# Two plain tiles ahead of the Strassen-like products in the second FFN pass

## What is computed

```python
x = x + gt1 * rms_norm(yx, norm_g[1])                   # yx: mLSTM output
h = rms_norm(x, norm_g[2]) * (1 + sc2) + sh2
u, g = split(h @ w_in)                                  # 1024 -> 2 x 2816
f = (silu(dwconv(g)) * u) @ w_out                       # 2816 -> 1024
x = x + gt2 * rms_norm(f, norm_g[3])
```

## Time and profile before

| | us |
|---|---|
| median of 3 runs (2484.39 to 2489.68) | 2487.13 |
| the profiled execution, its own time | 2494.55 |
| its span in the trace, first to last instruction | 2492.5 |
| PE busy / DVE / POOL / ACT | 2354.7 / 1742.9 / 875.3 / 815.7 |
| mean granted TensorE clock, share of full speed | 0.976 |

### The profile page before, as it was taken

The page is one execution under the profiler, slowest core; times in us unless marked ns, Lnnn a source line. Parts: engine busy times, 40 slices in busy tenths (PEclk is TensorE's granted clock), DMA queues, the critical chain, the costliest instruction groups (busy, mean ns, idle before and its releaser), DMA issues.

```text
span 2492.5 us, 36004 instructions
## 1 busy us (share of the span) xinstructions
PE 2354.7 (94%) x13606; PEld 1926.0 (77%) x13606; DVE 1742.9 (70%) x2193; ACT 815.7 (33%) x1182; POOL 875.3 (35%) x432
## 2 busy tenths in 40 slices
...
DMA packets 106689, 255.08 MB, mean 102 GB/s; under 512 B 8929, under 2 KB 62817, under 8 KB 92129
## 3 DMA queue, kind: packets, MB, share of 16 engines
...
## 4 chain that ended last, share of the span: by engine, by line
PE 78%; DVE 12%; ACT 4%; DMA 3%; issue 2%; POOL 1%; SPq 0%; ACTq 0%; DVEq 0%; POOLq 0%
PE ps L717 17%; PE ps L718 16%; PE ps L719 16%; PE ps L1365 4%; PE ps L1367 4%; PE ps L1366 4%; DVE acc L2822 3%; DVE y_x L2868 2%; PE ps L1115 2%; PE ps L1116 2%; PE ps L1117 2%; PE ps L1268 1%; PE ps L819 1%; PE ps L852 1%; PE ps L754 1%
## 5 line engine op out<-in xcount | busy, mean ns | idle before, releaser
L2953 POOL TENSOR_TENSOR w_lo<-raw,w_hi 128x2048 fp32r<-128x2048 f32 x57 | 266.8, 4681 | 653.0 <-ACT w_hi L1604 293.9
L717 PE MATMUL ps<-hx_hi,w_hi 128*128 128x512 f32 x848 | 338.7, 399 | 2.5 <-ACT mix_out_c L1758 1.0
L718 PE MATMUL ps<-hx_hi,w_lo 128*128 128x512 f32 x848 | 331.8, 391 | 0.0
L719 PE MATMUL ps<-hx_lo,w_hi 128*128 128x512 f32 x848 | 331.5, 391 | 0.0
L2333 DVE TENSOR_TENSOR y_x<-y_x,ps 128x1024 f32<-128x1024 f32 x176 | 214.7, 1221 | 63.0 <-PE ps L719 59.5
L2315 DVE SCALAR_TENSOR_TENSOR acc<-ps,fcv,acc 128x945 f32<-128x945 f32 (+2 forms) x176 | 215.0, 1222 | 37.4 <-ACT acc L1648 16.3
L2822 DVE SCALAR_TENSOR_TENSOR acc<-ps,fcv,acc 128x945 f32<-128x945 f32 (+2 forms) x176 | 215.0, 1222 | 18.6 <-ACT acc L2159 2.7
L2868 DVE TENSOR_TENSOR y_x<-y_x,ps 128x512 f32<-128x512 f32 x304 | 205.2, 687 | 14.1 <-PE ps L719 14.0
L717 PEld LDWEIGHTS ps<-hx_hi,w_hi 128*128 128x128 f32 x848 | 160.2, 189 | 40.3 <-DVE hx_lo L2470 2.5
L719 PEld LDWEIGHTS ps<-hx_lo,w_hi 128*128 128x128 f32 x848 | 160.1, 189 | 34.0
L718 PEld LDWEIGHTS ps<-hx_hi,w_lo 128*128 128x128 f32 x848 | 160.3, 189 | 30.6
...
## 6 DMA issues: line engine op xcount, KB each, us to landing
raw<-in_ffn_w SPq DMA_DIRECT2D x44, 1024.0 KB, 6.6
...
f_raw<-in_ffn_w SPq DMA_DIRECT2D x22, 1024.0 KB, 5.0
modw<-in_modw SPq DMA_DIRECT2D x21, 1024.0 KB, 4.8
raw<-in_mlstm_w SPq DMA_DIRECT2D x14, 1024.0 KB, 5.3
...
```

Of the source, the lines that this page charges most:

```text
L717: pe.matmul(out, whi, hhi, start=first, stop=False)
L718: pe.matmul(out, wlo, hhi, start=False, stop=False)
L719: return pe.matmul(out, whi, hlo, start=False, stop=last)
L2953: pool.tensor_tensor(w_lo[:, slot, 0:2048], raw[:, slot, 0:2048], w_hi[:, slot, 0:2048].bitcast(F32), ALU.subtract)\
```

## The change

The first two tiles are made plainly, with eight multiplications: `first_halves` runs the first token half of gate and up of both tiles (32 steps) while the second half is still being normed, with its sums of squares between them; `second_halves` follows when x12 and x22 exist (another 32 steps). The combinations t1 to t4 are made behind that, mostly on POOL, and are first used in tile 2, which takes the gate-first order and whose weight parts lie in swapped slots (THIRD_SLOT), since the plain tiles still hold the others. `free_at` takes these slots in. SP's first two loads of f_raw and the order of its others change with it. The low part of the gated product of tiles 1 to 20 goes from DVE (`f_low` in `f_tile`) to POOL (`gated_low` in `parts`, behind sum s4). Tile 21 takes the gate-first order. The semaphore bases are moved to fit; they are left out here, as are `plain` (one step: three matmuls of the same 128 x 512 form) and the functions that only take a new name for the order. The diff, cut, in the order SP, PE, ACT, DVE, POOL:

```diff
-FIRST_ORDER = ("g1", "g2", "s1", "s2", "s4", "s3", "u2")
+GATE_FIRST = ("g1", "g2", "s1", "s2", "s4", "s3", "u2")
 ORDER = ("g1", "s1", "s2", "s4", "s3", "g2", "u2")
-MADE_FIRST = FIRST_ORDER
+MADE_THIRD = ("s1", "u2", "g1", "g2", "s2", "s4", "s3")
+PLAIN = 2
...
+PLAIN_PARTS = (("g1", "g2", "s1", "s2"), ("a1", "a2", "b1", "b2"))
+PLAIN_GATE = (2, 0)
+PLAIN_UP = ((1, 1), (5, 4))
+THIRD_SLOT = {"g1": "g1", "g2": "g2", "u2": "u2", "s1": "s4", "s4": "s1", "s2": "s3", "s3": "s2"}
...
 def free_at(name):
-    return max(done_at(True, name), done_at(False, name))
-def made_at(first, name):
-    return (MADE_FIRST if first else ORDER).index(name) + 1
+    return max(done_at(True, name), done_at(True, THIRD_SLOT[name]), done_at(False, name))
...
+sp.dma_start(f_raw[:], a["ffn_w"][FT][:, 0:2048]).then_inc(sem("raw_in0"), 16)
 sp.wait_ge(sem("gated"), 8)
 sp.wait_ge(sem("mo_low"), 1)
 sp.wait_ge(sem("x_out"), 16 * KT)
 sp.dma_start(res_h[:], x_scr[1][:, :, 0:TH]).then_inc(sem("resh_in"), 16)
+sp.wait_ge(sem("lo_in"), PLAIN_LOW + 4)
+sp.dma_start(f_raw[:], a["ffn_w"][FT + 1][:, 0:2048]).then_inc(sem("raw_in0"), 16)
...
-halves_in(1)
-sp.wait_ge(sem("c_shifted"), SECOND["c_shifted"] + KH)
-sp.wait_ge(sem("pre_t"), SECOND["pre_t"] + 18)
+halves_in(2)
+sp.wait_ge(sem("post_done"), posts["x_mlstm"] + 16)
 out_in(0)
+sp.wait_ge(sem("c_shifted"), SECOND["c_shifted"] + 8)
+sp.wait_ge(sem("pre_t"), SECOND["pre_t"] + 2)
 mod_half(0)
-halves_in(2)
...
+def first_halves():
+    for step in range(4 * KT):
+        t, up, k = step // (2 * KT), step // KT % 2, step % KT
+        if step < KT:
+            pe.wait_ge(sem("pre_lo"), lows["x_pre2b"] + k + 1)
+        if k % KH == 0:
+            pe.wait_ge(sem("lo_in"), PLAIN_LOW + 4 * t + 2 * up + k // KH + 1)
+        if t and up and k == 0:
+            pe.wait_ge(sem("act_moved"), PLAIN_MOVED + 1)
+        plain(t, up, 0, k)
+        if step == 1:
+            half_sums("p", 3, KT - 1)
+        if step == 7:
+            pe.wait_ge(sem("sq_p"), 32)
+            half_spread("p", 3)
+        if 14 <= step <= 28 and step % 2 == 0:
+            half_sums("q", 3, (step - 14) // 2)
+    half_spread("q", 3)
+def second_halves():
+    for k in range(KT):
+        pe.wait_ge(sem("pre_lo"), lows["x_pre2b"] + 8 + k + 1)
+        plain(0, 0, 1, k)
+        plain(0, 1, 1, k)
+    pe.wait_ge(sem("act_moved"), PLAIN_MOVED + 2)
+    for k in range(KT):
+        plain(1, 0, 1, k)
+    for k in range(KT):
+        plain(1, 1, 1, k)
...
+    product("g1", made("g1"), third)
     if last:
         pe.wait_ge(sem("mod1_done"), FT)
-    product("g2", made("g2"))
-    pe.wait_ge(sem("dve_moved"), j * 3 + (SECOND["dve_moved"] + 2))
-    product("u2", made("u2"))
+    if third or last:
+        product("g2", made("g2"), third)
+    pe.wait_ge(sem("dve_moved"), j * 3 + (summed - 2))
+    if third:
+        pe.wait_ge(sem("pool_low"), SECOND["pool_low"] + 10)
+    product("s1", made("s1"), third)
+    pe.wait_ge(sem("act_moved"), j * 4 + (moved + 1))
+    if third:
+        pe.wait_ge(sem("pool_low"), SECOND["pool_low"] + 12)
+    product("s2", made("s2"), third)
+    pe.wait_ge(sem("act_moved"), j * 4 + (moved + 2))
+    product("s4", made("s4"), third)
+    pe.wait_ge(sem("act_moved"), j * 4 + (moved + 3))
+    if third:
+        pe.wait_ge(sem("pre_lo"), SECOND["pre_lo"] + 2)
+    product("s3", made("s3"), third)
+    if not (third or last):
+        pe.wait_ge(sem("dve_moved"), j * 3 + summed)
+        product("g2", made("g2"))
+    pe.wait_ge(sem("dve_moved"), j * 3 + (summed + (3 if third or last else 2)))
+    product("u2", made("u2"), third)
...
-first_products()
-products(1)
+first_halves()
+second_halves()
+pe.wait_ge(sem("act_moved"), PLAIN_MOVED + 3)
 down(0, 0, True)
+products(2, third=True)
+down(1, 1)
 with pe.Fori(0, FT // 2 - 2) as i:
-    products(i * 2 + 2)
-    down(i * 2 + 1, 1)
     products(i * 2 + 3)
     down(i * 2 + 2, 0)
-products(FT - 2)
-down(FT - 3, 1)
-products(FT - 1, True)
+    products(i * 2 + 4)
+    down(i * 2 + 3, 1)
+products(FT - 1, last=True)
...
-part_high("g1", 0, True)
-part_high("g2", 0, True)
+for n in range(4):
+    plain_high(0, n)
 for d in range(KT):
     copy_out(0, d)
-    if d == 2:
-        part_high("s1", 0, True)
-        part_high("s2", 0, True)
...
+for n in range(4):
+    plain_high(1, n)
 for d in range(KT):
     keep(posts["x_mlstm"], 3, d)
+    if d == 3:
+        plain_moved(0, 0)
 half_deviation("q", 3)
+plain_moved(1, 0)
+for k in range(KH):
+    act.activation(y_x[:, KH + k, 0:TH], y_x[:, KH + k, 0:TH], ACT.Identity, bias=shift(1, 1, "x", KH + k)).then_inc(sem("c_shifted"), 1)
+for d in range(KH):
+    high1(d)
+act.wait_ge(sem("x_out1"), 32 * KT)
+for k in range(KH):
+    high1(KH + k)
+    act.activation(x12_at[:, k, :], res_h[:, k, :], ACT.Identity, bias=shift(1, 1, "x", k)).then_inc(sem("c_shifted"), 1)
+for k in range(KH):
+    act.wait_ge(sem("pre_lo"), lows["x_pre2b"] + 12 + k + 1)
+    act.activation(x22_at[:, k, :], x22_at[:, k, :], ACT.Identity, bias=shift(1, 1, "x", KH + k)).then_inc(sem("c_shifted"), 1)
+part_high("s1", 2, True)
+part_high("u2", 2, True)
+out_high(0)
+plain_moved(0, 1)
+plain_gate(0)
 for k in (0, 2):
+    act.wait_ge(sem("pre_t"), SECOND["pre_t"] + 1 + k // 2)
+    pair_high("t1", k, x_val["t1"])
+part_high("g1", 2, True)
+part_high("g2", 2, True)
 for k in (0, 2):
+    act.wait_ge(sem("pool_low"), SECOND["pool_low"] + 1 + k // 2)
+    pair_high("t2", k, x_val["t2"])
+act.wait_ge(sem("w_in_used"), PLAIN_DONE + 7)
 for k in (0, 2):
+    act.wait_ge(sem("pool_low"), SECOND["pool_low"] + 3 + k // 2)
+    pair_high("t3", k, x12_at)
+act.wait_ge(sem("tap_done"), SECOND["tap_done"] + 8)
+act.activation(acc[:], acc[:], ACT.Silu).then_inc(sem("silu_done"), 1)
+plain_moved(1, 1)
+act.wait_ge(sem("a_done"), SECOND["a_done"] + 1)
+act.activation(fa_hi[:], fprod[:, 0, :], ACT.Copy).then_inc(sem("a_hi_ready"), 1)
 for k in (0, 2):
+    act.wait_ge(sem("pool_low"), SECOND["pool_low"] + 5 + k // 2)
+    pair_high("t4", k, x22_at)
+plain_gate(1)
+for name in ("s2", "s4", "s3"):
+    part_high(name, 2, True)
...
-def f_tile(j, par, adds=True, mod_half=None):
+def f_tile(j, par, mod_half=None):
     f_taps(j - 1)
     gate_second(j)
     f_gate(j - 1, 1 - par)
     up_second(j, par)
-    f_low(j - 1, 1 - par)
-    gate_first(j)
+    gate_first_half(j)
     if mod_half is not None:
         last_mod_half(mod_half)
-    if adds:
-        f_add(j - 1)
-gate_second(0, True)
-up_second(0, 0, True)
-gate_first(0)
-f_taps(0)
+    f_add(j - 1)
+f_taps(0, PLAIN_GATE[0])
 f_gate(0, 0)
 f_low(0, 0)
-gate_second(1)
-up_second(1, 1)
-gate_first(1)
-dve.wait_ge(sem("x_out1"), 32 * KT)
+for k in (0, 2):
+    dve.wait_ge(sem("pre_hi"), SECOND["pre_hi"] + 5 + k // 2)
+    if k == 0:
+        dve.wait_ge(sem("w_in_used"), PLAIN_DONE + 8)
+    dve.tensor_tensor(x_lo["t3"][:, k:k + 2, :], x12_at[:, k:k + 2], x_hi["t3"][:, k:k + 2, :].bitcast(F32), ALU.subtract)\
+        .then_inc(sem("pre_lo"), 1)
+dve.wait_ge(sem("pre_lo"), SECOND["pre_lo"] + 2)
 f_add(0, True)
-with dve.Fori(0, 6) as i:
-    f_tile(i * 2 + 2, 0)
+f_taps(1, PLAIN_GATE[1])
+gate_first_half(2, True)
+f_gate(1, 1)
+gate_second(2, True)
+up_second(2, 0, True)
+f_add(1)
+with dve.Fori(0, 5) as i:
     f_tile(i * 2 + 3, 1)
-for j in range(14, FT - 1):
-    f_tile(j, j % 2, mod_half=j - 14 if j < 20 else None)
-f_tile(FT - 1, 1, adds=False)
+    f_tile(i * 2 + 4, 0)
+for j in range(13, FT - 1):
+    f_tile(j, j % 2, mod_half=j - 14 if 14 <= j < 20 else None)
+f_taps(FT - 2)
+gate_first_half(FT - 1, True)
+f_gate(FT - 2, 0)
+gate_second(FT - 1, True)
+up_second(FT - 1, 1, True)
 f_taps(FT - 1)
...
+def part_sum(name, j, third=False):
+    if third and name in ("s1", "s2"):
+        pool.wait_ge(sem("r_p" if name == "s1" else "r_q"), 4)
+    elif third:
+        pool.wait_ge(sem("w_in_used"), PLAIN_DONE + 6)
+    else:
         pool.wait_ge(sem("w_in_used"), j * 7 + (SECOND["w_in_used"] + free_at(name) - 7))
-    one, two, op = {"s1": (part("u1"), part("u2"), ALU.add), "s2": (p_val["s1"][:], part("g1"), ALU.subtract),
-                    "s4": (part("g2"), p_val["s2"][:], ALU.subtract), "s3": (part("g1"), part("u1"), ALU.subtract)}[name]
...
+def gated_low(j, par):
+    pool.wait_ge(sem("a_hi_ready"), j + (SECOND["a_hi_ready"] + 1))
+    pool.tensor_tensor(fa_lo[:, par, :], fprod[:, par, :], fa_hi[:].bitcast(F32), ALU.subtract).then_inc(sem("a_lo_ready"), 1)
+def parts(j, par):
     part_low("g1", j)
-    if between is not None:
-        between()
+    out_low(j - 2)
     part_sum("s1", j)
     part_sum("s2", j)
     part_low("s1", j)
     part_sum("s4", j)
+    gated_low(j - 2, par)
     part_low("s2", j)
...
+for t in range(PLAIN):
+    for n in range(4):
+        plain_low(t, n)
+part_sum("s1", 2, True)
+part_sum("s2", 2, True)
+part_low("s1", 2, True)
+part_low("u2", 2, True)
+out_low(0)
+for k in (0, 2):
+    pool.wait_ge(sem("pre_t"), SECOND["pre_t"] + 1 + k // 2)
```

(44 more changed lines are left out.)

338 lines of the change are left out of this document (124 added, 214 removed).

## The result

The changed kernel takes **2571.02 us** (median, 2564.77 to 2571.58), the kernel before 2487.36 beside it: ratio **1.0332 [1.0317, 1.0347]**, 83.7 us slower. The forecast was 2551 us, range 2520 to 2586. The profiled execution is 2571.05 us with a span of 2569.1, 76.6 over the span of before.

What follows compares the result with a forecast made beforehand. PE, busy 94% of the span, was taken as the bound, so any new gap costs in full. 92 - 9.5 - 17 - 1.3 = +64 us gave 2558.6 profiled, 2551 us against the median; range 2520 to 2586 us.

Steps and rivals of the forecast that it cites:

- Step 1, the later release: Tiles from 3 on: late s1 sum delays silu and up_second; PE waits 3.5 us for u2, plus 1.5 us low clock.
- Step 2, the low part on POOL: Low part behind POOL's sums holds the down projection until 2071.2, not 2066.07; with the release 5.1 us a tile, +92 us.
- the two ways reckoned: POOL's low part done at 2069.9 without the DVE/POOL port lock, or 2071.2 if each waits out the other's whole instructions.
- Both chains meet there: Why 5.1 us a tile was taken: u2 ends at 2071.1 and POOL's low part at 2071.2, just before the down projection.
- The low clock: u2's matmuls run slower after PE's wait: 1.5 us a tile, from one 2.94 us gap; 5 us at the seam.
- both stalls pay for the clock: Rival, chance 0.17: PE waits again and the slow stretch falls into the down projection; 6.7 us a tile, 2580 us.
- Step 3, DVE relieved: Six tiles with a mod half lose DVE's 1.58 us excess each, as DVE has less work: -9.5 us.
- Step 4, the seam: From mLSTM output to tile 3's products: 115.1 us instead of 132.5, with 30.3 us of stalls; -17 us, bounds -5 and -28.
- Step 5: The end: gate-first order in tile 21 lets ACT's 1.27 us run while DVE waits for s3; -1.3 us, bounds 0 and -2.
- The loads: SP's first two f_raw loads, moved later, cost nothing at the seam; uncovered, 5 us each.
- The median: Sum made against the profiled execution, 2494.6 us, giving 2558.6; 7.4 us taken off for the median, giving 2551 us.

Runs made afterwards that it cites:

- e1: Changed kernel with the later counts (s1 after product 5, s2 after product 6) for tile 3 alone, later tiles by the old counts: 2487.3 us, ratio 1.0000.
- e2: Kernel before with the later counts alone (s1 after product 5, s2 after product 6), low part still on DVE: 2600.1 us, ratio 1.0455.
- e8: Changed kernel, later counts kept, with silu and the gated product's high and low parts moved ahead in ACT's and POOL's queues: 2468.1 us, ratio 0.9918.
- e3: e1 with s1 released after product 5 and s2 still after product 4, tiles 4 to 21: 2559.8 us, ratio 1.0287.
- e4: e1 with s2 released after product 6 and s1 still after product 3, tiles 4 to 21: 2570.1 us, ratio 1.034.
- e5: e1 with the low part of the gated product back on DVE, behind up_second: 2471.0 us, ratio 0.9935.
- e6: e1, low part on POOL, with the mod half split in two pairs, one ahead of gate_first_half and one behind: 2461.2 us, ratio 0.9893.
- e11: e8 with e6's mod-half split, and the first load of f_raw back in the mLSTM scan as before the change: 2459.6 us, ratio 0.9889.

## Why the prediction was right, and where not

**Step 1, the later release: right.** On the distance from the fifth product's end, forecast and measured: sum s1 0.32 and 0.33 us, silu 2.27 and 2.27, f_gate 3.57 and 3.53, up_second 5.5 and 5.3, u2 6.3 and 6.1, the down projection 10.57 and 10.56. e1 and e2 show that the counts are the cause, e8 that they act through the queues.

**Step 2, the low part on POOL: right for the period.** It is done at 10.11 us on that scale, between the 9.3 and 10.6 of the two ways reckoned; the rows follow the second (whole instructions), a bit sooner because f_gate was. That it costs nothing behind u2 held, but for two tiles (below). "Both chains meet there" held more strongly than I wrote it: e3 and e4. But I had the chain behind s2 only on POOL; e4 shows that it also runs over ACT, where fa_hi stands behind the high part of s2.

**The low clock: mis-sized.** The granted clock from 1867 to 2440 is 0.94 against 1.00 before, so the loss is there as forecast. The forecast took 1.5 us a tile from one case. 8 of the 11 periods are 35.05 to 35.20 us and fit; three are 36.27 to 36.47. Two stretches of after with such a wait, first from a short period and then from a long one (busy time of PE, PEld, DVE, ACT, POOL, then PEclk, DMA share, GB/s):

```profile
1937.00:1944.00 7.00, 4.97 (x15) 3.92 (x16) 2.51 (x3) 3.73 (x5) 7.00 (x5) 0.76 0.00 0
1973.00:1980.00 7.00, 5.78 (x14) 4.53 (x15) 1.69 (x3) 3.19 (x5) 7.00 (x5) 0.54 0.00 0
```

PE stood 3.2 us both times. In the first it was granted the low level, 1.2 GHz (0.43 us a matmul against 0.23), from the third matmul after it went on; in the second from the first matmul, and for longer. By the starts of the matmuls the low level cost 1.6 to 1.8 us in seven of the eleven tiles and 2.9 to 3.0 in three. In the eleventh (u2 at 2080.92) it cost 0.3, u2 ended early, and PE stood another 1.2 us for POOL's low part. That is +4 us over the eleven periods. The rival "both stalls pay for the clock" came out nearer in its number (2580) than in its mechanism: only two waits for fa_lo are in the list, and the first of these two tiles took 35.1 us, not the rival's 36.7.

**Step 3, DVE relieved: wrong.** This is the step that failed. I counted DVE's work in these tiles (30.4 us in a period of 35) and took the whole 1.58 us a tile as won, as if no wait for the additions were left. But the additions wait for the end of the mod half, whatever the sum. Before, the half began 3.8 us behind up_second (low part between them) and was over 8.0 us behind it (2282.36 - 2274.32):

```profile
2274.32 0.69 DVE L2849 TENSOR_TENSOR fprod<-fprod,ps 128x512 f32<-128x512 f32 x1 [0.21 <-PE ps L1367]
2275.32 2.29 DVE L2835 TENSOR_TENSOR fa_lo<-fprod,fa_hi 128x1024 fp32r<-128x1024 f32 x1 [0.31 <-ACT fa_hi L2130]
...
2279.01 3.35 DVE L2297 SCALAR_TENSOR_TENSOR macc_x<-modh,c_pad,macc_x 128x256 f32<-128x256 f32 x3
```

After, it begins 1.2 us behind up_second and is over 8.0 us behind it all the same (2338.40 - 2330.41, in the chain under e5 and e6): POOL's work, with the moved instruction in it, stretches it by the time that the move had freed. So PE waits 1.2 us for the additions in four of these six tiles, much as before (1.3), and the tiles cost +5.0 us each, not +3.5. In e1, where up_second isn't held up, gate_first_half makes the half wait for g2 besides (2.03 us), it is over 9.0 us behind up_second, and the forecast relief of 9.5 us is a loss of 15 (six times 34.2 - 31.7). e5 and e6 undo it in two ways.

**Step 4, the seam: right in kind, 4.7 us short.** PE's waits in after, 1721 to 1850:

```profile
PE ps L733 <- issue: 11.5, 1, 11.5
PE ps L1367 <- DVE fprod L2881: 3.8, 1, 3.8
PE ps L1377 <- DVE x_lo L2536: 3.6, 1, 3.6
PE ps L733 <- DVE y_x L2903: 3.3, 1, 3.3
PE ps L1367 <- ACT fprod L2212: 2.1, 1, 2.1
```

The first row, for which the profile names no releaser, is down(0). Forecast were 10.8 (down(0)), 3.9 (u2), 3.7 (root), 3.4 (additions) and 3.5 (weights of tile 3): 25.3 against 24.3 us. What was short is the clock. The same view of after at the seam:

```profile
1789.00:1800.00 11.00, 7.65 (x19) 5.71 (x20) 9.83 (x7) 1.11 (x2) 11.00 (x4) 0.68 0.00 0
...
1825.00:1836.00 11.00, 7.23 (x22) 5.39 (x22) 3.38 (x3) 4.99 (x6) 9.51 (x7) 0.74 0.00 1
```

PE busy times the missing share is 2.4 and 1.9 us here, and in six such stretches from 1727.8 to 1847.8 together 7.8, not 5. The remaining 2.9 us lie in PE's own work as I counted it, and I have not split them; they are no larger than the 3 us by which the same seam differs from run to run (above).

**Step 5: its gain did not come. The loads: nothing, as forecast.** The wait ahead of the last down projection is 4.2 us (first list) and was 6.65 before. But u2 of tile 21 now waits 0.8 us, and from PE's start of tile 21 to the end of the span it is 75.8 us against 75.4, so the forecast -1.3 us came out as +0.4; I have not split the rest. e11 shows the early load to be free.

**The median.** Medians are 83.7 us apart and profiled executions 76.5, as the one of before was 7.4 over its median; I made the sum against it and then took the 7.4 off, which was right. Of the 20 us that were missing, 13 are the loop (9 step 3, 4 clock), 5 the seam, 2 tile 20 and the end.
